# Stick-breaking attention with queries on partitions, a reversed scan in place of suffix-sum products

## Chip, cores and metric

One core of a Trainium2 chip runs the whole program. The metric is the device time of one execution in microseconds. The kernel before took 2721.27 us (median of 3 runs, 2720.59 to 2722.27).

## What is computed

The program is a chain of transformer-like layers on 512 tokens of width 1024, all in float32. The change touches one of them, the stick-breaking attention of the last mixer: 16 heads of 64 dimensions, 512 queries and keys.

```python
def stick_breaking_attention(q, k, v):
    """A[t,s] = beta_ts * prod_{s<j<t}(1 - beta_tj), s < t."""
    for i in range(seq // Q_BLOCK):              # blocks of 128 queries
        z = einsum('bqhd,bkhd->bhqk', q_block, k[:, :kv_len]) * scale
        causal = k_pos < q_pos
        log_beta = log_sigmoid(z)
        log_1m = where(causal, log_beta - z, 0.0)
        later = cumsum(log_1m, axis=3, reverse=True) - log_1m
        w = where(causal, exp(log_beta + later), 0.0)
        out = einsum('bhqk,bkhd->bqhd', w, v[:, :kv_len])
```

The weight of a key is its own sigmoid times the product of (1 - sigmoid) over all later keys before the query.

## The kernel before

The program is written engine by engine. A list of stages (`plan`) is made first, and each engine walks the list in order, issuing its own instructions and waiting on counted semaphores (`wait_ge(*at_(...))`, raised by `.then_inc(*by(...))`). Every engine runs its instructions strictly in that order, so a waiting instruction holds all that is behind it on its engine.

Most stages are large matrix products, three products on split float32 values each (L1760 to L1762), whose weights SyncE loads two units ahead, ScalarE rounds (L985) and VectorE subtracts (L1394). The attention stage `attend` stands between two of them (the query projection and the product with `b_w_o`); both weight buffers are then full, so it runs with no weight traffic.

The attention has keys on partitions. Head by head, for key blocks j = 0 to 3, with 512, 384, 256 and 128 queries (1280 columns):

- TensorE makes the scores in one of four PSUM banks `X` (L1986). A bank is taken when its last user has been read (`bank`, `freed`).
- VectorE adds the causal bias and moves them to SBUF (L1574).
- ScalarE runs Abs, Exp and Ln over all 1280 columns (L1239, L1240, L1247), each Exp and Ln with a change of its function table.
- VectorE makes softplus and log beta (L1586, L1587).
- TensorE adds up the softplus of later keys: `below` for the keys of the same block (L1996), a tile of ones for each later block (L1999), into PSUM `G`: ten fp32 products a head.
- VectorE subtracts that from log beta (L1580), ScalarE takes Exp (L1244), TensorE multiplies with the values (L2008), VectorE copies the head's output (L1591).

Heads are staggered over a loop index k: in one turn TensorE issues the scores of head k+1, the suffix sums of k-1 and the value products of k-2. An fp32 product appears as two MATMUL records in the trace; a transpose appears as one.

The constants `ident`, `upper` and `below` are made by GpSimd at the start (L915 to L929). GpSimd's work during the projections is the squares for the norms (L952). It has none in the attention. The stage after, `down`, starts when the last head's output is in `big`: ScalarE makes `u_hi` (L1263), VectorE `u_lo` (L1702).

Of the kernel before, what the change touches and what calls it, by code (L numbers as in the profile page):

```python
# [12 lines left out]
P = 128  # L13
# [114 lines left out]
def build(nc, w, out, upto=None):  # L128
# [3 lines left out]
    with ExitStack() as ctx:  # L132
# [22 lines left out]
        below = sb("below", [P, P])  # L155
# [240 lines left out]
        def plan_sb():  # L396
            s = stage("attend", akind="SB", heads=SB_HEADS, aux={}, operand=state["operand"])
            use = s.aux
            s.gfreed = [gfreed[m][-1] for m in range(4)]
            for k in range(-1, s.heads + 3):  # L400
                if k + 1 < s.heads:
                    for j in range(TT):
                        use["qk", k + 1, j] = aux("z", s.i, k + 1, j)
                        mark("z", s.i, k + 1, j)
                    mark("log_done", s.i, k + 1)
                if 1 <= k <= s.heads:
                    mark("sp", s.i, k - 1)
                    for j in range(TT):
                        mark("later", s.i, k - 1, j)
                        mark("arg", s.i, k - 1, j)  # L410
                if 2 <= k < s.heads + 2:
                    mark("exp_done", s.i, k - 2)
                    use["pv", k - 2] = aux("y", s.i, k - 2)
                    mark("y", s.i, k - 2)
            state["y"] = ("y", s.i, s.heads - 1)

# [216 lines left out]
        plan_sb()  # L633
        plan_down(8)
# [193 lines left out]
        def _(pool):  # L828
# [65 lines left out]
            def pool_s5_table():  # L894
# [7 lines left out]
                for n in (2, 4, 8, 16, 32):  # L902
# [14 lines left out]
            pool.memset(below[:, :], 1.0).then_inc(consts, 1)  # L917
            pool.wait_ge(consts, 3)
# [7 lines left out]
            pool.wait_ge(consts, 7)  # L926
            pool.tensor_copy(bias_tile[:, :], junk[:, 1, :].bitcast(I32)).then_inc(consts, 1)
            pool.wait_ge(consts, 8)
# [4 lines left out]
            for n in range(NUSED):  # L933
# [22 lines left out]
        tri_at, TRI = [0, 512, 896, 1152], 1280  # L956
        workf = work[:, :, :].rearrange("p a b -> p (a b)")

        def tri(x, j=None):
            return x[:, 0:TRI] if j is None else x[:, tri_at[j]:tri_at[j] + SEQ - P * j]  # L960

        def sb_sp(hd, j=None):
            return tri(att[:, 16:21, :].rearrange("p a b -> p (a b)")[:, TRI * (hd % 2):TRI * (hd % 2) + TRI], j)

        def sb_lb(hd, j=None):
            x = workf[:, TRI:2 * TRI] if hd % 3 == 2 else \
                big[:, 16:21, :].rearrange("p a b -> p (a b)")[:, TRI * (hd % 3):TRI * (hd % 3) + TRI]
            return tri(x, j)

        def sb_z(hd, j=None):  # L970
            return tri(workf if hd % 2 else att[:, 21:24, :].rearrange("p a b -> p (a b)"), j)
# [3 lines left out]
        def _(act):  # L975
# [25 lines left out]
            def act_slot(s, t):  # L1001
# [6 lines left out]
                if s.akind == "s5":  # L1008
                    return act_s5(s, t)
                maps, T = 2 if s.akind == "A" else 1, len(s.steps)  # L1010
# [133 lines left out]
            act.wait_ge(consts, 9)  # L1144
# [3 lines left out]
            for s in plan:  # L1148
# [83 lines left out]
                elif s.kind == "attend":  # L1232
                    for k in range(s.heads + 2):
                        if k < s.heads:
                            L = sb_lb(k)
                            if k >= 3:
                                act.wait_ge(*at_("aux_ready", s.aux["pv", k - 3]))
                            act.wait_ge(*at_("z", s.i, k, TT - 1))
                            link("act", act, nc.scalar.activation(L, sb_z(k), ACT.Abs))  # L1239
                            link("act", act, nc.scalar.activation(L, L, ACT.Exp, scale=-1.0))  # L1240
                        if k >= 2:
                            act.wait_ge(*at_("arg", s.i, k - 2, TT - 1))
                            e = sb_lb(k - 2)
                            nc.scalar.activation(e, e, ACT.Exp).then_inc(*by("exp_done", s.i, k - 2))  # L1244
                        if k < s.heads:

                            nc.scalar.activation(L, L, ACT.Ln, bias=one_c).then_inc(*by("log_done", s.i, k))  # L1247
# [39 lines left out]
        def _(dve):  # L1287
# [136 lines left out]
            def dve_slot(s, t):  # L1424
# [6 lines left out]
                if s.akind == "s5":  # L1431
                    return dve_s5(s, t)
                T = len(s.steps)
# [128 lines left out]
            def dve_sb(s):  # L1562

                link("dve", dve, V.tensor_scalar(bias_tile[:, :], upper[:, :], -BIG, BIG, ALU.mult, ALU.add))
                link("dve", dve, V.scalar_tensor_tensor(bias_tile[:, 0:P], ident[:, :], BIG, bias_tile[:, 0:P],
                                                        ALU.mult, ALU.add))
                for k in range(s.heads + 3):
                    if k < s.heads:
                        if k >= 2:
                            dve.wait_ge(*at_("sp", s.i, k - 2))  # L1570
                        for j in range(TT):
                            a = s.aux["qk", k, j]
                            dve.wait_ge(*at_("aux_ready", a))
                            V.tensor_tensor(sb_z(k, j), X[:, a % 4, 0:SEQ - P * j], bias_tile[:, 0:SEQ - P * j],  # L1574
                                            ALU.add).then_inc(*by("z", s.i, k, j))
                    if 2 <= k < s.heads + 2:
                        for j in range(TT):
                            e = sb_lb(k - 2, j)
                            dve.wait_ge(*at_("later", s.i, k - 2, j))
                            V.tensor_tensor(e, e, G[:, j, 0:SEQ - P * j], ALU.subtract)\  # L1580
                                .then_inc(*by("arg", s.i, k - 2, j))
                    if 1 <= k <= s.heads:

                        z, L = sb_z(k - 1), sb_lb(k - 1)
                        dve.wait_ge(*at_("log_done", s.i, k - 1))
                        link("dve", dve, V.scalar_tensor_tensor(sb_sp(k - 1), z, 0.0, L, ALU.max, ALU.add))  # L1586
                        V.scalar_tensor_tensor(L, z, 0.0, L, ALU.min, ALU.subtract).then_inc(*by("sp", s.i, k - 1))  # L1587
                    if k >= 3:
                        a, r = s.aux["pv", k - 3], 64 * ((k - 3) % 2)
                        dve.wait_ge(*at_("aux_ready", a))  # L1590
                        V.tensor_copy(big[r:r + 64, (k - 3) // 2, :], X[r:r + 64, a % 4, :])\  # L1591
                            .then_inc(*by("y", s.i, k - 3))
# [3 lines left out]
            for s in plan:  # L1596
# [81 lines left out]
                elif s.kind == "attend":  # L1678
                    dve_sb(s)
# [70 lines left out]
        def _(pe):  # L1750
# [22 lines left out]
            def pe_slot(s, t):  # L1773
# [6 lines left out]
                if s.akind == "s5":  # L1780
                    return pe_s5(s, t)
                T = len(s.steps)
# [35 lines left out]
                if t < T:  # L1818
# [4 lines left out]
                    for m in range(2 if s.akind == "A" else 1):  # L1823
# [10 lines left out]
                        ins.then_inc(*by("aux_ready", s.aux["qk", t, m]))  # L1834

# [63 lines left out]
            pe.wait_ge(consts, 9)  # L1899
# [8 lines left out]
            for s in plan:  # L1908
# [68 lines left out]
                elif s.kind == "attend":  # L1977
                    pe.wait_ge(*at_(*s.operand))
                    vv = att[:, 0:8, :].rearrange("p (t a) n -> p t (a n)", a=2)
                    for k in range(-1, s.heads + 2):  # L1980
                        if k + 1 < s.heads:
                            hd = k + 1
                            r = slice(64 * (hd % 2), 64 * (hd % 2) + 64)
                            for j in range(TT):
                                b = bank(s.aux["qk", hd, j])
                                pe.matmul(b[:, 0:SEQ - P * j], big[r, 8 + hd // 2, j * P:(j + 1) * P],  # L1986
# [58 lines left out]
```

## Time and profile before

| what | value |
|---|---|
| median of 3 runs | 2721.27 us |
| profiled execution | 2723.9 us, span 2722.2 us |
| TensorE busy | 2468.2 us, 91% |
| VectorE busy | 1397.0 us, 51% |
| ScalarE busy | 972.3 us, 36% |
| GpSimd busy | 226.3 us, 8% |
| chain that ended last | TensorE 83%, VectorE 9%, issue 3%, ScalarE 3% |
| mean granted TensorE clock | 0.944 |

The shares are averages over the whole program. The attention stage is 167 us of it, and its engines are loaded otherwise than the average; it has to be read by itself, from the stretch 2118 to 2286 us of the span. The granted clock is a share of 2.4 GHz: 1.00 is full speed, 0.50 is 1.2 GHz.

### The profile page before, as it was taken

The numbers are of one execution on the slowest core, as the hardware profiler recorded it, in microseconds if no ns is written. First come the engines' busy times: TensorE is split into PE (matmuls) and PEld (weight loads), VectorE is DVE, ScalarE is ACT, GpSimd is POOL, SyncE is SP. The second block draws the span as 40 slices with busy tenths as digits, with TensorE's granted clock in tenths as the row PEclk, the third lists the DMA queues.
The fourth block names the chain that finished last, engine by engine and source line by source line (L and its number), as shares of the span: only waits on it lengthen the run. The fifth ranks groups of instructions, "written<-read, shape, count | busy, mean of one in ns | idle before, by whom it ended". The sixth has DMA issues, their size and how long they took to land.

```text
span 2722.2 us, 29106 instructions
## 1 busy us (share of the span) xinstructions
PE 2468.2 (91%) x11110; PEld 1945.3 (71%) x11110; DVE 1397.0 (51%) x2851; ACT 972.3 (36%) x1312; POOL 226.3 (8%) x252
## 2 busy tenths in 40 slices
PE   4789989898799999999798989999899899899998
PEld 3567667677577676767687778878687556688877
DVE  6875575755445343443364354554444675445543
ACT  3334435332443434342313222223333775222232
POOL 6531010042010000000000000000011000000000
PEclk9889999899799999989877999999999899899999
DMA  6344112124132121214362222222222000233222
GB/s 170 111 135 124 62 48 76 47 93 139 62 93 63 62 78 47 78 47 147 117 212 67 93 78 93 93 93 83 88 89 82 1 1 31 77 94 93 93 78 93
DMA packets 191358, 233.46 MB, mean 86 GB/s; under 512 B 39455, under 2 KB 120822, under 8 KB 191222
## 3 DMA queue, kind: packets, MB, share of 16 engines
q1 hardware_dynamic: 170503, 211.05, 24.3%
q10 hardware_dynamic: 20719, 20.56, 2.5%
q8 instruction: 90, 1.47, 0.2%
q14 instruction: 46, 0.38, 0.0%
HBM read 212.69 MB, written 23.07 MB: 87 GB/s over the span
## 4 chain that ended last, share of the span: by engine, by line
PE 83%; DVE 9%; issue 3%; ACT 3%; SPq 1%; DMA 1%; ACTq 0%; POOLq 0%; DVEq 0%
PE G L1760 22%; PE G L1761 21%; PE G L1762 21%; PE X L1880 2%; PE X L1915 2%; PE G L1996 1%; ACT w_hi L985 1%; PE G L1999 1%; PE X L2008 1%; PE X L1816 1%; PE X L1769 1%; PE X L1830 1%; PE X L1986 1%; DVE w_lo L1394 1%; PE X L1804 1%
## 5 line engine op out<-in xcount | busy, mean ns | idle before, releaser
L1394 DVE TENSOR_TENSOR w_lo<-raw,w_hi 128x512 fp32r<-128x512 f32 x696 | 481.8, 734 | 613.0 <-ACT w_hi L985 612.7
L1760 PE MATMUL G<-w_hi,u_hi 128*128 128x512 f32 x1600 | 653.5, 408 | 23.2 <-issue 14.8
L1762 PE MATMUL G<-w_hi,u_lo 128*128 128x512 f32 x1600 | 633.7, 396 | 0.0
L1761 PE MATMUL G<-w_lo,u_hi 128*128 128x512 f32 x1600 | 633.3, 396 | 0.0
L985 ACT ACTIVATE w_hi<-raw 128x2048 fp32r<-128x2048 f32 (+1 forms) x176 | 333.5, 1895 | 837.6 <-PE G L1762 796.9
L1760 PE MATMUL G<-u_hi,w_hi 128*128 128x512 f32 x1120 | 450.6, 402 | 0.0
L1761 PE MATMUL G<-u_lo,w_hi 128*128 128x512 f32 x1120 | 441.8, 394 | 0.0
L1762 PE MATMUL G<-u_hi,w_lo 128*128 128x512 f32 x1120 | 441.1, 394 | 0.0
L1760 PEld LDWEIGHTS G<-w_hi,u_hi 128*128 128x128 f32 x1600 | 307.4, 192 | 108.5 <-issue 35.1
L1762 PEld LDWEIGHTS G<-w_hi,u_lo 128*128 128x128 f32 x1600 | 306.2, 191 | 67.2
L1761 PEld LDWEIGHTS G<-w_lo,u_hi 128*128 128x128 f32 x1600 | 307.5, 192 | 61.7 <-issue 0.5
L1760 PEld LDWEIGHTS G<-u_hi,w_hi 128*128 128x128 f32 x1120 | 213.6, 191 | 64.5 <-issue 18.4
L1762 PEld LDWEIGHTS G<-u_hi,w_lo 128*128 128x128 f32 x1120 | 213.5, 191 | 46.4
L1761 PEld LDWEIGHTS G<-u_lo,w_hi 128*128 128x128 f32 x1120 | 214.0, 191 | 42.3
L952 POOL TENSOR_TENSOR work<-att 128x512 f32<-128x512 f32 x68 | 76.6, 1127 | 1661.9 <-ACT att L990 1661.8
L1702 DVE TENSOR_TENSOR u_lo<-big,u_hi 128x512 fp32r<-128x512 f32 x132 | 86.3, 718 | 158.8 <-ACT u_hi L1263 158.8
L1915 PE MATMUL X<-ident,att 128*128 128x128 f32 x256 | 48.6, 370 | 101.9 <-DVE att L1603 99.4
L1915 PEld LDWEIGHTS X<-ident,att 128*128 128x128 f32 x256 | 43.7, 197 | 107.6 <-DVE att L1603 102.4
L1042 ACT ACTIVATE att<-att,small 128x128 f32<-128x128 f32 (+3 forms) x112 | 62.5, 559 | 131.0 <-DVE small L1461 130.9
L1024 ACT ACTIVATE att<-X 128x128 f32<-128x128 f32 (+2 forms) x112 | 46.9, 419 | 134.9 <-PE X L1816 134.9
L1816 PE MATMUL X<-ident,att 128*128 128x128 f32 x264 | 49.1, 280 | 37.7 <-DVE work L1490 21.5
L1457 DVE CUSTOM_DVE_ANT_0 att<-X,bias_tile 128x128 f32<-128x128 f32 (+3 forms) x48 | 23.5, 489 | 108.7 <-PE X L1830 108.7
(292 smaller groups left out, 2472.3 us busy)
## 6 DMA issues: line engine op xcount, KB each, us to landing
raw<-in_ffn_w_up SPq DMA_DIRECT2D x88, 512.0 KB, 4.7
raw<-in_e_w_in SPq DMA_DIRECT2D x56, 512.0 KB, 4.7
raw<-in_o_w_in SPq DMA_DIRECT2D x56, 512.0 KB, 4.5
raw<-in_ffn_w_down SPq DMA_DIRECT2D x40, 512.0 KB, 4.6
raw<-in_e_w_out SPq DMA_DIRECT2D x16, 512.0 KB, 4.5
raw<-in_o_w_out SPq DMA_DIRECT2D x16, 512.0 KB, 4.5
raw<-in_a_w_glu SPq DMA_DIRECT2D x16, 512.0 KB, 4.0
raw<-in_w_kv SPq DMA_DIRECT2D x16, 512.0 KB, 4.3
```

Source lines behind the costliest of these rows:

```text
L952: pool.tensor_tensor(sq[:, m, :], x, x, ALU.mult).then_inc(*by("q_squared", s.i, m))
L985: nc.scalar.activation(w_hi[:, n % HL, 0:kn], raw[:, n % RAW, 0:kn], ACT.Copy).then_inc(w_hi_done, 1)
L1024: nc.scalar.activation(att[:, 20:20 + nb, i * P:(i + 1) * P], X[:, a % 4, 0:nb * P].rearrange("p (a b) -> p a b", b=P), ACT.Copy).then_inc ...
L1042: ins = nc.scalar.activation(S, src, ACT.Exp, bias=nmx[:, c:c + 1], accum_out=rs[:, c:c + 1])
L1394: V.tensor_tensor(w_lo[:, n % HL, k], raw[:, n % RAW, k], w_hi[:, n % HL, k].bitcast(F32), ALU.subtract).then_inc(w_lo_done, 1)
L1702: V.tensor_tensor(u_lo[:, 4 * (l % 2) + j, :], big[:, k, :], u_hi[:, 4 * (l % 2) + j, :].bitcast(F32), ALU.subtract).then_inc(*by("u_ready ...
L1760: pe.matmul(out, lh, rh, start=start, stop=False)
L1761: pe.matmul(out, lh, rl, start=False, stop=False)
L1762: return pe.matmul(out, ll, rh, start=False, stop=stop)
L1816: ins = pe.transpose(b[:, j * P:(j + 1) * P], S[:, j * P:(j + 1) * P], ident[:, :])
L1880: ins = pe.matmul(b[a][:, NSUP * g + 1:NSUP * g + NSUP], Z[r, c, g, :], S[r, c, g, 0:NSUP - 1], start=False, stop=g == 3 and c == 1)
L1915: ins = pe.transpose(b[:, t * P:(t + 1) * P], xn_view[:, t, k * P:(k + 1) * P], ident[:, :])
```

## The change

Queries lie on partitions, keys on columns. There are 64 steps of (head, block i of 128 queries), over L = 128 (i+1) keys. ScalarE takes two Sigmoids of the scores straight from PSUM: of -z (`sb_keep`, 1 minus beta) and of z (`sb_take`, beta). VectorE runs `tensor_tensor_scan` from the last key to the first, state = max(keep x state, bias); the bias is 0 except in the diagonal block, where it is 1 at and after the query. GpSimd zeroes beta at and after the query in the diagonal block. VectorE multiplies beta by the product of the next key on. TensorE transposes the weights block by block into `G`, ScalarE copies them to SBUF, and after a head's fourth step TensorE multiplies with the values and VectorE copies the output. The suffix-sum products, `below`, Abs, Exp, Ln and the bias additions are gone.

The stage is now of kind `between` with a host of 69 slots. In slot t the queues are: TensorE scores of t, transposes of t-3, value products if t-4 is a head's last step; ScalarE both Sigmoids of t, copy of t-3; VectorE scan and product of t, output copy if t-5 is a last step; GpSimd the select of t.

```diff
-        below = sb("below", [P, P])
+        def sb_keep(t):
+            return att[:, 16 + t % 3, :]
+        def sb_prod(t):
+            return work[:, 4 + t % 2, :]
+        def sb_take(t):
+            return big[:, 16 + t % 4, :]
+        def sb_turned(hd):
+            return work[:, 0:4, :] if hd % 2 else att[:, 20:24, :]
 @block.gpsimd
-            pool.memset(below[:, :], 1.0).then_inc(consts, 1)
-            pool.affine_select(out=below[:, :], in_=below[:, :], compare_op=ALU.is_gt, fill=0.0, base=0,
-                               pattern=[[-1, P]], channel_multiplier=1).then_inc(consts, 1)
+                if n == sb_down.n:
+                    for t, (hd, i) in enumerate(sb_mix.steps):
+                        d = sb_take(t)[:, P * i:P * i + P]
+                        pool.wait_ge(*at_("sb_take", sb_mix.i, t))
+                        pool.affine_select(out=d, in_=d, compare_op=ALU.is_gt, fill=0.0, base=0, pattern=[[-1, P]],
+                                           channel_multiplier=1).then_inc(*by("sb_masked", sb_mix.i, t))
+            def act_sb(s, t):
+                T = len(s.steps)
+                if t < T:
+                    hd, i = s.steps[t]
+                    a, L = s.aux["qk", t], P * (i + 1)
+                    act.wait_ge(*at_("aux_ready", a))
+                    if t >= 3:
+                        act.wait_ge(*at_("sb_product", s.i, t - 3))
+                    nc.scalar.activation(sb_keep(t)[:, 0:L], X[:, a % 4, 0:L], ACT.Sigmoid, scale=-1.0)\
+                        .then_inc(*by("sb_keep", s.i, t))
+                    if t >= 4:
+                        act.wait_ge(*at_("sb_turned", s.i, t - 4))
+                    nc.scalar.activation(sb_take(t)[:, 0:L], X[:, a % 4, 0:L], ACT.Sigmoid)\
+                        .then_inc(*by("sb_take", s.i, t))
+                if 0 <= t - 3 < T:
+                    hd, i = s.steps[t - 3]
+                    if hd >= 2 and i == 0:
+                        act.wait_ge(*at_("aux_ready", s.aux["pv", hd - 2]))
+                    act.wait_ge(*at_("sb_turned", s.i, t - 3))
+                    nc.scalar.activation(sb_turned(hd)[:, 0:i + 1, i * P:(i + 1) * P],
+                                         G[:, (t - 3) % 4, 0:(i + 1) * P].rearrange("p (a b) -> p a b", b=P),
+                                         ACT.Copy).then_inc(*by("pt_copied", s.i, t - 3))
+            def dve_sb(s, t):
+                T = len(s.steps)
+                if t == 0:
+                    link("dve", dve, V.memset(bias_tile[:, 0:384], 0.0))
+                    link("dve", dve, V.tensor_copy(bias_tile[:, 384:512], upper[:, 0:P]))
+                if t < T:
+                    i = s.steps[t][1]
+                    L = P * (i + 1)
+                    dve.wait_ge(*at_("sb_keep", s.i, t))
+                    V.tensor_tensor_scan(sb_prod(t)[:, 0:L][:, ::-1], sb_keep(t)[:, 0:L][:, ::-1],
+                                         bias_tile[:, 384 - P * i:512][:, ::-1], 1.0, ALU.mult, ALU.max)\
+                        .then_inc(*by("sb_product", s.i, t))
+                    dve.wait_ge(*at_("sb_product", s.i, t))
+                    dve.wait_ge(*at_("sb_masked", s.i, t))
+                    w_ = sb_take(t)[:, 0:L - 1]
+                    V.tensor_tensor(w_, w_, sb_prod(t)[:, 1:L], ALU.mult).then_inc(*by("p_ready", s.i, t))
+                if is_last(s, t - 5):
+                    hd = s.steps[t - 5][0]
+                    a, q = s.aux["pv", hd], 64 * (hd % 2)
+                    dve.wait_ge(*at_("aux_ready", a))
+                    V.tensor_copy(big[q:q + 64, hd // 2, :], X[q:q + 64, a % 4, :]).then_inc(*by("y", s.i, hd))
+            def pe_sb(s, t):
+                T = len(s.steps)
+                if t < T:
+                    hd, i = s.steps[t]
+                    b, L = bank(s.aux["qk", t]), P * (i + 1)
+                    r = slice(64 * (hd % 2), 64 * (hd % 2) + 64)
+                    pe.matmul(b[:, 0:L], att[r, 8 + hd // 2, i * P:(i + 1) * P], big[r, 8 + hd // 2, 0:L],
+                              start=True, stop=True).then_inc(*by("aux_ready", s.aux["qk", t]))
+                if 0 <= t - 3 < T:
+                    i = s.steps[t - 3][1]
+                    pe.wait_ge(*at_("p_ready", s.i, t - 3))
+                    pe.wait_ge(*at_("sb_masked", s.i, t - 3))
+                    pe.wait_ge(*(at_("pt_copied", s.i, t - 7) if t >= 7 else at_(*s.gfreed[t - 3])))
+                    for j in range(i + 1):
+                        ins = pe.transpose(G[:, (t - 3) % 4, j * P:(j + 1) * P], sb_take(t - 3)[:, j * P:(j + 1) * P],
+                                           ident[:, :])
+                    ins.then_inc(*by("sb_turned", s.i, t - 3))
+                if is_last(s, t - 4):
+                    hd = s.steps[t - 4][0]
+                    pe.wait_ge(*at_("pt_copied", s.i, t - 4))
+                    b = bank(s.aux["pv", hd])
+                    for j in range(TT):
+                        ins = pe.matmul(b[r, P * j:SEQ], vv[:, j, 64 * hd:64 * hd + 64], sb_turned(hd)[:, j, P * j:SEQ],
+                                        start=j == 0, stop=j == TT - 1)
+                    ins.then_inc(*by("aux_ready", s.aux["pv", hd]))
```

## Rows read from the trace of the kernel before

**Rows 1.** Windows of the attention stage: window, length, busy us (instructions) per engine, PEclk, DMA, GB/s.
```profile
core 0: us, PE busy (x) PEld busy (x) DVE busy (x) ACT busy (x) POOL busy (x), PEclk, DMA share, GB/s
2118.66:2285.92 167.26, 152.77 (x576) 92.11 (x576) 113.71 (x176) 124.90 (x97) 0.00 (x0) 0.96 0.00 1
2147.99:2262.10 114.11, 111.76 (x426) 67.64 (x427) 83.41 (x132) 92.88 (x72) 0.00 (x0) 0.99 0.00 1
```

**Rows 2.** Chain of waits in one steady head: start, us, what, records.
```profile
2244.75 2.35 PE X L1986 x8
2247.10 1.05 PE G L1996 x2
...
2250.76 0.43 PE G L1996 x2
2251.64 2.30 PE X L2008 x8
```

**Rows 3.** The same chain, transposes before the stage and a table load.
```profile
2107.19 0.45 PE X L1769 x4
...
2114.21 3.69 PE X L1769 x16
...
2122.89 1.28 ACT L1240
```

**Rows 4.** Groups of instructions by form: count, busy us, mean ns, idle before.
```profile
L1024 ACT ACTIVATE att<-X 128x512 f32<-128x512 f32 x20 | 11.9, 597 | 33.2 <-PE X L1816 33.2
L1024 ACT ACTIVATE att<-X 128x128 f32<-128x128 f32 x20 | 5.5, 277 | 53.0 <-PE X L1816 53.0
L1229 ACT ACTIVATE att<-G 128x256 f32<-128x256 f32 x16 | 6.1, 384 | 29.7 <-PE G L1762 29.7
L1051 ACT ACT_TABLE_LOAD x1 | 1.3, 1283 | 9.8 <-issue 9.8
L1580 DVE TENSOR_TENSOR big<-big,G 128x512 f32<-128x512 f32 x11 | 7.6, 688 | 17.7 <-PE G L1999 17.7
L1580 DVE TENSOR_TENSOR big<-big,G 128x128 f32<-128x128 f32 x11 | 3.1, 279 | 0.0
L921 POOL TENSOR_SCALAR_AFFINE_SELECT upper<-upper 128x512 f32<-128x512 f32 x1 | 0.6, 612 | 0.0
L923 POOL TENSOR_SCALAR_AFFINE_SELECT below<-below 128x128 f32<-128x128 f32 x1 | 0.3, 292 | 0.0
L1880 PE MATMUL X<-work,att 64*128 64x63 f32 x256 | 43.1, 375 | 0.0
```

**Rows 5.** Single lines: duration in ns as least, median, most, and first and last start.
```profile
L1690 DVE TENSOR_TENSOR_SCAN big<-att x1: 1212/1212/1212, 745.2 to 745.2; 12x512 f32<-12x512 f32 x1
L952 POOL TENSOR_TENSOR work<-att x68: 1038/1040/1557, 61.0 to 2109.0; 128x512 f32<-128x512 f32 x68
```

**Rows 6.** Timeline: start, us of the merged run, engine, line, operation, count.
```profile
1363.25 1.42 DVE L1543 TENSOR_TENSOR_SCAN work<-big,work 128x256 f32<-128x256 f32 x2
2099.35 2.13 DVE L1394 TENSOR_TENSOR w_lo<-raw,w_hi 128x512 fp32r<-128x512 f32 x2
2099.39 1.55 POOL L952 TENSOR_TENSOR work<-att 128x512 f32<-128x512 f32 x1 [13.58 <-ACT att L990]
2285.23 0.69 DVE L1591 COPY big<-X 64x512 f32<-64x512 f32 x1 [1.18 <-PE X L2008]
2286.62 4.91 DVE L1702 TENSOR_TENSOR u_lo<-big,u_hi 128x512 fp32r<-128x512 f32 x8 [0.69 <-ACT u_hi L1263]
```

**Rows 7.** Windows of two stretches at a lower granted clock, columns as in rows 1.
```profile
2176.00:2184.00 8.00, 7.61 (x22) 4.19 (x21) 4.95 (x8) 7.69 (x6) 0.00 (x0) 0.79 0.01 1
1404.00:1460.00 56.00, 51.19 (x323) 49.79 (x323) 25.10 (x42) 9.35 (x16) 0.00 (x0) 0.50 0.40 118
```

**Rows 8.** Windows before, during and after sixteen transposes, columns as in rows 1.
```profile
2111.00:2114.20 3.20, 0.00 (x0) 0.00 (x0) 2.83 (x13) 0.00 (x0) 0.00 (x0) 0.51 0.00 0
2114.20:2117.90 3.70, 3.68 (x16) 3.27 (x16) 2.39 (x5) 2.06 (x3) 0.00 (x0) 0.50 0.00 0
2118.00:2122.00 4.00, 3.34 (x12) 1.94 (x13) 1.89 (x5) 1.00 (x2) 0.00 (x0) 1.00 0.00 0
```

More of the change, by code:

```diff
@@ L396, in plan_sb, with plan_sb_slot @@
         def plan_sb():
-            s = stage("attend", akind="SB", heads=SB_HEADS, aux={}, operand=state["operand"])
-            use = s.aux
+            s = Stage("attend", akind="SB", heads=SB_HEADS, aux={}, operand=state["operand"])
+            s.i = ("attention", "SB", len(plan))
+            s.steps = [(hd, i) for hd in range(s.heads) for i in range(TT)]
+            s.slots = len(s.steps) + 5
             s.gfreed = [gfreed[m][-1] for m in range(4)]
[L400 to L414, printed above, removed]
-            state["y"] = ("y", s.i, s.heads - 1)
+            stage("between", host=s, host_at=0, host_end=s.slots)
+            for t in range(s.slots):
+                plan_sb_slot(s, t)
+            state["y"] = ("y", s.i, s.heads - 1)
+            return s
+        def plan_sb_slot(s, t):
+            T = len(s.steps)
+            if t < T:
+                s.aux["qk", t] = aux("sb_take", s.i, t)
+                mark("sb_keep", s.i, t)
+                mark("sb_take", s.i, t)
+                mark("sb_masked", s.i, t)
+                mark("sb_product", s.i, t)
+                mark("p_ready", s.i, t)
+            if 0 <= t - 3 < T:
+                mark("sb_turned", s.i, t - 3)
+                mark("pt_copied", s.i, t - 3)
+            if is_last(s, t - 4):
+                hd = s.steps[t - 4][0]
+                s.aux["pv", hd] = aux("y", s.i, hd)
+                mark("y", s.i, hd)
         def plan_down(kt, first=0, host=None, host_at=0, y=None):
@@ L1231, in _ @@
                         w_high(n + 2)
[L1232 to L1247, printed above, removed]
                 elif s.kind == "forget":
@@ L1560, in dve_s5 @@
                         .then_inc(*by("u_ready", s.i, k))
[L1562 to L1592, printed above, removed]
@@ L1781, in pe_slot @@
                     return pe_s5(s, t)
+                if s.akind == "SB":
+                    return pe_sb(s, t)
                 T = len(s.steps)
@@ L1976, in _ @@
                     ins.then_inc(*by("aux_ready", s.aux))
[L1977 to L1986, printed above, removed]
-                                          att[r, 8 + hd // 2, j * P:SEQ], start=True, stop=True)\
-                                    .then_inc(*by("aux_ready", s.aux["qk", hd, j]))
-                        if 1 <= k <= s.heads:
-                            g = k - 1
-                            pe.wait_ge(*at_("sp", s.i, g))
-                            for j in range(TT):
-                                pe.wait_ge(*at_(*(("arg", s.i, g - 1, j) if g else s.gfreed[j])))
-                                b = G[:, j, :]
-                                ins = pe.matmul(b[:, 0:SEQ - P * j], below[:, :], sb_sp(g, j), start=True,
-                                                stop=j == TT - 1)
-                                for i in range(j + 1, TT):
-                                    ins = pe.matmul(b[:, P * (i - j):SEQ - P * j], ones[:, :], sb_sp(g, i),
-                                                    start=False, stop=i == TT - 1)
-                                ins.then_inc(*by("later", s.i, g, j))
-                        if k >= 2:
-                            g = k - 2
-                            pe.wait_ge(*at_("exp_done", s.i, g))
-                            b = bank(s.aux["pv", g])
-                            r = slice(64 * (g % 2), 64 * (g % 2) + 64)
-                            for j in range(TT):
-                                ins = pe.matmul(b[r, P * j:SEQ], vv[:, j, 64 * g:64 * g + 64], sb_lb(g, j),
-                                                start=j == 0, stop=j == TT - 1)
-                            ins.then_inc(*by("aux_ready", s.aux["pv", g]))
                 elif s.kind == "between":
```

43 lines of the change are left out of this document (22 added, 21 removed).

## The prediction
> **What bounds the kernel now.** I read the page's shares first (TensorE 91% busy, 83% of the chain of waits), then windows of the one stage that the change rewrites, then the chain inside it. The stage runs from the first score product at 2118.66 to the end of the last head's output copy at 2285.92: 167.26 us, of which TensorE is busy 152.77, ScalarE 124.90, VectorE 113.71, GpSimd 0, with no DMA to speak of [rows 1]. In its steady part TensorE is busy 111.76 of 114.11 us, and those twelve heads give 9.51 us a head. The chain there is TensorE's own sequence [rows 2]: four score products (eight records) 2.35 us; the suffix sums, from 2247.10 to the start of the value products at 2251.64, 4.54 us; the value products 2.30 us; every second head a 0.7 us wait of the score products for a bank that VectorE's copy frees. So TensorE bounds this stage, and nearly half of its time there is the suffix sums. What lies around the 16 heads is the filling (no TensorE work in some of 2119 to 2146) and the emptying (2262 to 2286).
>
> **What goes, what comes, on each engine.** Per head, four steps of 128 queries against 128, 256, 384 and 512 keys, 1280 columns in all, as many as before.
>
> *TensorE.* Gone: 10 fp32 products (20 records) for the suffix sums, 4.54 us. The score and value products keep their shapes and counts (only which operand is stationary changes), 2.35 and 2.30 us. New: 1+2+3+4 = 10 transposes of 128x128. The trace has the same operation: four take 0.45 us at full clock, 0.11 each, and sixteen take 3.69 us at half clock, 0.23 each [rows 3]. Ten cost 1.1 us. Sum: 2.35 + 2.30 + 1.1 = 5.75 us a head.
>
> *ScalarE.* Gone: per head four passes over 1280 columns and two table loads of 1.28 us. New: three passes over the four pieces, two Sigmoids and one copy, all read from PSUM, and no table change between them. Such a pass takes 0.277 us for 128 columns and 0.597 for 512, and a Sigmoid of 256 columns 0.384, on the same line [rows 4]; the four pieces sum to 1.75 us, three times that is 5.2 us. One table load remains, at the first Sigmoid.
>
> *VectorE.* Gone: the bias additions, the subtractions and the two 1.49 us passes per head. New: per step one scan, a wait for it, and one product. The trace has the scan at 512 columns (1.212 us, on 12 partitions) and at 256 columns on 128 partitions, where two linked ones take 1.42 us, thus 0.69 each with 0.036 between [rows 5, 6]: 2.04 ns a column. Four: 0.43 + 0.69 + 0.95 + 1.21 = 3.28, with links 3.43 us. A two-input product takes 0.279 us at 128 and 0.688 at 512 columns, and eight of 512 without a wait take 4.91 us, a pitch of 0.60, 0.083 below the duration [rows 4, 6]. Four products cost 1.93 - 4 x 0.083 = 1.60 us; the output copy, 0.69 us long [rows 6], costs 0.60 at that pitch. Sum 5.63 us a head. That the scan reads and writes backwards appears in no row: I bound it by no change below and by twice the scan, 2.6 us more a head, above; I take no change, since the row nearest is a scan of the same types, and keep the other end as a rival.
>
> *GpSimd.* New: one select on 128x128 per step, 0.292 us when alone [rows 4]; 1.2 us a head, far from a bound. But it shares something with VectorE. GpSimd's square of 128x512 takes 1.04 us at the median; the one at 2099.39, issued while VectorE ran a two-input subtraction, took 1.55 us, and the VectorE pair around it took 2.13 us where two at that pitch take 1.29: VectorE lost 0.84 us, about as long as the square's own columns, and GpSimd lost 0.5, the rest of VectorE's instruction [rows 5, 6]. Both new VectorE operations have two SBUF inputs. A select streams 128 columns; from 0.292 us for 128 and 0.612 for 512 columns its own columns take 0.107 us [rows 4]. So I charge VectorE 4 x 0.107 = 0.43 us a head. Bounds: 0 (it falls into the gap between scan and product), and 4 x 0.292 = 1.17. VectorE then needs 6.06 us a head, and it is the new bound, with TensorE 0.3 behind and ScalarE 0.8 behind.
>
> **Does the order of the queues let VectorE run through?** Slots are 3 deep. VectorE's product of step t needs the select of t, behind both Sigmoids of t; ScalarE's Sigmoids of t stand behind its copy of step t-4, which needs TensorE's transposes of t-4, which need VectorE's product of t-4. Worst place: TensorE's value products (2.30 us) stand ahead of the next head's 128-query scores and of the transposes of its second step. From the end of the product of step 0 of a head: transposes and value products until 2.5, score 2.8, first Sigmoid 3.2; VectorE comes to that scan only after steps 1, 2, 3 and the copy, 5.3 us. About 2 us to spare; the steps of 256, 384 and 512 keys have as much or more. GpSimd waits at most one scan (1.2 us) for its turn and still comes before the product. The output copy needs the value products 3.2 us after the same instant and stands behind some 5 us of work. So what is late next is VectorE alone. TensorE waits for it about 1 us in one stretch of each head. I still allow 0.15 us a head, 2.4 us, for waits between queues.
>
> **The stage after.** Filling: score of 128 queries 0.5, table load 1.28, Sigmoid 0.28, passing between engines 0.2: 2.25 us until VectorE starts (the table load as it appears in the chain [rows 3]). Then 16 x 6.06 - 0.60 = 96.4. Emptying: transposes 0.65 with passing, copy 0.7, value products 2.4, output copy 0.75: 4.5. With the allowance 105.5 us, against 167.3: 61.8 less.
>
> **The rest.** A memset and the select of `below` (0.29 us) leave GpSimd's first 5 us; ScalarE's first table load only comes after 9.8 us in which nothing of GpSimd holds it [rows 4], so nothing is gained, 0.5 us at most. The 64 selects stand in GpSimd's queue behind the last squares, with nothing behind them. The bias preparation stays two small VectorE operations before the scores. SyncE has nothing to move here: both weight buffers are full before the stage. The next stage starts from the last output copy as before.
>
> The sum goes by the profiled execution: 2723.9 (span 2722.2 and 1.7 around it) - 61.8 = 2662.1. The median of the runs, 2721.3, lies 2.6 below the profiled one: 2659.5, so 2660.
>
> **Rivals.** (a) *TensorE's clock sinks once in each head.* The work that remains is score products on 64 rows, value products on 64 columns, and transposes, with a wait of about 1 us a head. For: before, between 2176 and 2184, the clock was 0.79 with TensorE busy 7.61 of 8 us, and from 1404 to 1460 it stayed at 0.50, the 1.2 GHz level, with TensorE busy 51.2 of 56 us, with products of 64 and 63 columns [rows 4, 7]. Against: it was 0.99 over the steady 114 us [rows 1], and transposes raised it: 0.51 in the idle stretch before them, 0.50 during 3.7 us of nothing else, 1.00 right after [rows 8]. A mean of 0.79 over those 8 us is 3.4 us at half clock, which costs 1.7 us of TensorE time; one such stretch in every head, less the 0.3 to spare, 1.4 x 16 = 22 us: 2682.
>
> (b) *VectorE is dearer.* The backward scan at twice the time: 16 x 2.6 = 42 us, 2702. The select at 0.292 each instead of 0.107: 0.74 x 16 = 12 us, 2672.
>
> (c) *Slower: TensorE at 1.2 GHz throughout the stage.* Then 2 x 5.75 = 11.5 us a head, TensorE is the bound again, 184 + some 9 at the ends = 193 us, 26 more than before: 2747. It turns slower from about 10 us a head, a half-clock share of some 85% of the stage. Against: with TensorE the bound it would have no waits, and full columns follow each other, the condition in which the clock rose in rows 8; the stretch at 1404 had half as many columns to each weight load.
> The Trainium skill, "TensorE: Matmul & The Clock Gate", Part 4 (PE-mode transpose), says that transposes do not count as TensorE activity and so do not engage the full clock. By it each head would have 1.1 us more of "idle" beside its wait, which speaks for (a), or at worst (c), and the sum would be 2682 or 2747. The trace disagrees in the one place that shows transposes alone, the sixteen of rows 3 and 8, and I follow the trace.
>
> (d) *Cheaper.* Selects wholly hidden and no waits: 7 + 2.4 us less, 2650.
>
> **Chances.** Forecast (2650 to 2668) 0.60; (a) 0.18; (b) 0.12; (c) 0.04; (d) below 2650 0.04; a mishap that leaves the time within 0.2% of before 0.02. The range for 8 in 10 takes the forecast, (a) and the cheap half of (b): 2648 to 2690. A change under 0.2% (5.4 us) couldn't be told from none. Faster 0.94, within 0.01, slower 0.05.
>
> **What would show it.** In the new profile: the stage at about 105 us; VectorE busy over 95% of its steady part, scans of 1.21 us at 512 columns (2.3 would be (b)); some products or scans 0.1 us longer where a select runs; TensorE about 0.9 busy with short waits for VectorE's product, its clock near 1.0 (under 0.85 would be (a)); ScalarE about 85%. Wrong would be a chain in which TensorE or ScalarE holds most of the stage, or scans that wait for a Sigmoid in every step.

## The result, and the profile after

The changed kernel took 2671.26 us (median of 4 runs, 2666.25 to 2674.13) against 2721.77 before (four runs by now): ratio 0.9814, 95% interval 0.9801 to 0.9827. The profiled execution took 2668.6 us, span 2666.8. I had said 2660, range 2648 to 2690.

The stage first. It runs from the first score product at 2112.22 to the end of the last output copy at 2232.23, 120.0 us, where [rows 1] had 167.3 and I had said 105.5. Windows of the changed kernel (columns as in rows 1): the low-clock stretch around the stage's start, and its steady part.

```profile
core 0: us, PE busy (x) PEld busy (x) DVE busy (x) ACT busy (x) POOL busy (x), PEclk, DMA share, GB/s
2103.50:2130.80 27.30, 22.25 (x54) 11.65 (x55) 16.32 (x35) 12.58 (x27) 4.70 (x9) 0.50 0.00 1
2130.80:2225.00 94.20, 94.20 (x355) 44.29 (x356) 78.50 (x123) 60.87 (x166) 35.31 (x55) 1.00 0.00 1
```

In the steady part TensorE is busy all 94.20 us, VectorE 78.50 (83%), ScalarE 60.87. TensorE still bounds the stage; I had named VectorE. Before the steady part the granted clock is 0.50 for 27 us, 18.6 of them inside the stage. The chain of waits over one steady head answers to rows 2:

```profile
2158.08 0.41 PE X L1858 x2
2158.49 0.37 PE G L1866 x2
2158.86 0.62 PE X L1858 x2
2159.49 0.48 PE G L1866 x3
2159.97 0.84 PE X L1858 x2
2160.80 0.59 PE G L1866 x4
2161.39 1.05 PE X L1858 x2
2162.45 0.26 PE G L1866
2162.71 2.30 PE X L1876 x8
```

L1858 are the scores, L1866 the transposes, L1876 the value products. One head is 6.93 us (6.92 as a mean of many): scores 0.41 + 0.62 + 0.84 + 1.05 = 2.92 where [rows 2] had 2.35 for the same eight records, transposes 0.37 + 0.48 + 0.59 + 0.26 = 1.70 for ten where I had 1.1 from [rows 3], value products 2.30 as before. The step from one score group to the next is 0.21 us, the price of 128 columns; what is left in each is 0.20. The transposes are 0.11 each and 0.15 on top in each group. So each time TensorE goes from one kind of product to the other it loses 0.15 to 0.20 us, eight times a head, 1.4 us, of which the one switch into the scores (0.2) was already in my 2.35. A ninth one, into the value products, is in their 2.30, as it was before: their columns alone need 2.13.

The timeline shows where the loss sits. The weight loads (PEld) at two such switches of the changed kernel come first. Below them is the switch from value products to scores in the kernel before, load and product:

```profile
2165.72 0.29 PEld L1858 LDWEIGHTS X<-big,att 64*128 64x128 f32 x2 [0.17 <-issue]
2166.34 0.31 PEld L1866 LDWEIGHTS G<-ident,big 128*128 128x128 f32 x3 [0.33 <-issue]
```
```profile
2206.65 0.29 PEld L1986 LDWEIGHTS X<-att,big 64*128 64x128 f32 x2 [0.17 <-issue]
2206.66 0.69 PE L1986 MATMUL X<-att,big 64*128 64x512 f32 x1
```

The load starts with its product and not ahead of it (2206.65 and 2206.66): the weight load stands on the path. The tile shape, rows by columns of the weights, changes there: from 128 by 64 to 64 by 128 at this last switch, and between 64 by 128 and 128 by 128 at the two above. The Trainium skill, "TensorE: Matmul & The Clock Gate", Part 2 (what each phase is for), says that TensorE pulls a weight load ahead of the running product when the row groups don't conflict or the load goes to the background buffer. The traces agree with it inside a group of one shape: four transposes in a row take 0.11 us each with loads of 0.14 us. At a change of shape they show no pull-ahead.

VectorE's operations, and GpSimd's select, by form (mean ns after the busy us):

```profile
L1592 DVE TENSOR_TENSOR_SCAN work<-att,bias_tile 128x512 f32<-128x512 f32 x16 | 19.5, 1219 | 1.5 <-ACT att L1067 1.4
L1592 DVE TENSOR_TENSOR_SCAN work<-att,bias_tile 128x256 f32<-128x256 f32 x16 | 11.8, 737 | 0.2
L1598 DVE TENSOR_TENSOR big<-big,work 128x511 f32<-128x511 f32 x16 | 11.1, 692 | 3.1 <-POOL big L975 3.1
L975 POOL TENSOR_SCALAR_AFFINE_SELECT big<-big 128x128 f32<-128x128 f32 x64 | 40.8, 639 | 82.4 <-ACT big L1071 82.4
```

The backward scan takes 1.22 us at 512 columns, as the forward one of [rows 5] did. The select takes 639 ns in the mean where it took 292 alone [rows 4]. One that starts beside a scan shows why:

```profile
2163.25 1.22 DVE L1592 TENSOR_TENSOR_SCAN work<-att,bias_tile 128x512 f32<-128x512 f32 x1
2163.64 0.92 POOL L975 TENSOR_SCALAR_AFFINE_SELECT big<-big 128x128 f32<-128x128 f32 x1 [0.97 <-ACT big L1071]
```

It ends at 2164.56, 0.09 us after the scan; the one beside the scan of 384 columns ends 0.09 us after that, too.

Of the 55.4 us between the two spans, 47.3 are the stage, 1.7 what follows it, and 6.4 lie ahead of it, in code that the change touches only by the two instructions of `below`. That part is taken up under `e_below`.

### The profile page after: what moved, and what is told of

Read it like the earlier page. It is cut to its first block, busy times and chain, and to the rows that moved or that the text cites. A ratio compares the mean times of both kernels' runs of the same rounds, so it can differ in the third digit from the quotient of the medians.

```text
span 2666.8 us, 29121 instructions
## 1 busy us (share of the span) xinstructions
PE 2428.4 (91%) x10950; PEld 1905.4 (71%) x10950; DVE 1380.5 (52%) x2819; ACT 921.4 (35%) x1408; POOL 267.7 (10%) x314
## 4 chain that ended last, share of the span: by engine, by line
PE 84%; DVE 8%; issue 3%; ACT 3%; SPq 1%; DMA 1%; ACTq 0%; POOL 0%; DVEq 0%; POOLq 0%
PE G L1771 23%; PE G L1773 22%; PE G L1772 22%; PE X L1858 2%; PE X L1924 2%; PE X L1959 2%; PE X L1876 1%; ACT w_hi L991 1%; PE X L1829 1%; PE X L1780 1%; PE X L1843 1%; PE G L1866 1%; PE X L1846 1%; PE X L1817 1%; PE X L1842 1%
```

## The experiments

The theory after the first trace: TensorE loses an unhidden weight load at each change of tile shape, and starts the stage at half clock. Heads below are the spacing of the output copies in the steady part, stages go from first score to the end of the last copy. In the cuts of the edits `...` stands for lines left out.

**The changed kernel again, and with the unused tile back.** `a_same` is the same program; `e_below` differs by

```diff
+        below = sb("below", [P, P])
...
+            pool.memset(below[:, :], 1.0).then_inc(consts, 1)
+            pool.affine_select(out=below[:, :], ...).then_inc(consts, 1)
...
```

> The changed kernel itself, run again. In its first trace the attention takes 120 us: 16 heads at 6.93 us with TensorE busy throughout, and a first stretch to 2130.8 at half clock, which I put at some 7 us. Theory A (the low clock at the start of the stage is chance of when the clock rises): the time spreads over several us from run to run, 2664 to 2675, and the low stretch at the start has another length in this trace. Rival (the spread comes from elsewhere): the start of the stage looks the same and the time differs in another place.

> The changed kernel with the unused tile `below` back: its place in SBUF, its memset and its select. The changed kernel reached the attention 6.4 us earlier than the kernel before, 0.7 of it at the first weights, though nothing else in front of the stage was changed. Theory (the two GpSimd instructions stand on the starting path, and the rest is the clock falling and rising at other moments): first weights 0.7 us later again, and the attention starts somewhere within some us of the kernel before's. Rival (chance from run to run): the start of the attention differs from the first trace by as much in the unchanged program.

Measured: 2669.17 (2661.86 to 2671.84) and 2671.10 (2668.66 to 2673.76). Both heads 6.92, both stages 119.7 us, both at half clock for 23.9 us, from 1.5 us ahead of the last transposes before the stage. The first score came at 2116.0 and at 2113.1, where it was 2112.2 in the first trace and 2118.7 before. So `below` is not the cause, neither of the 6.4 us nor of the earlier first weights (with it back, they came 1.2 us before the old time); in the seven traces with the changed kernel's code ahead of the stage the first score comes between 2112.2 and 2118.0 (`e_pairs`), so that the old 2118.7 lies hardly outside of what one code shows. Against my expectation for `a_same` the low stretch at the start was nearly the same (27.3 and 23.9 us) and the stage the same to 0.3 us; the difference between the two traces lies ahead of the stage. The time is to be read by medians and the stage by itself.

**Scores over 128 rows.** `e_rows128`:

```diff
-                    r = slice(64 * (hd % 2), 64 * (hd % 2) + 64)
+                    r = slice(0, 128)
```

> The score products read all 128 rows of the query and key tiles instead of the head's 64 (the scores are then the sum of two heads', so the output is not the reference's). Columns and records are the same. Theory (TensorE loses 0.15 to 0.20 us of unhidden weight load each time when consecutive products differ in their rows or columns, 64x128 against 128x128, eight times a head): the head falls from 6.93 to about 5.6 us of TensorE work, VectorE becomes the bound at 6.1 to 6.3, the stage loses 10 to 13 us: 2658. Rival 1 (the loss comes from the switch between product and transpose, whatever the shape): nothing changes, 6.93 a head. Rival 2 (the loss comes from the semaphore waits ahead of each group): nothing changes either.

Measured: 2654.81 (2653.12 to 2656.46), ratio 0.9755 (0.9740 to 0.9769), head 6.09, stage 102.2. The chain over one head:

```profile
2154.49 0.42 PE X L1858 x2
2154.91 0.22 PE G L1866 x2
2155.13 0.43 PE X L1858 x2
2155.56 0.33 PE G L1866 x3
2155.89 0.65 PE X L1858 x2
2156.54 0.44 PE G L1866 x4
2156.97 0.04 issue
2157.01 1.13 PE X L1858 x2
2158.13 0.11 PE G L1866
```

In every other head the chain leaves TensorE once:

```profile
2148.36 0.43 PE X L1858 x2
...
2148.82 0.28 ACT att L1067
2149.10 0.18 ACT big L1071
...
2149.33 0.47 POOL big L975
...
2149.90 0.30 DVE big L1598
...
2150.22 0.69 DVE big L1605
...
2150.96 1.13 PE X L1858 x2
```

Two transposes 0.22, three 0.33, four 0.44, one 0.11: nothing is lost between products and transposes once both are 128x128. The first scores, behind value products of 64 columns, still cost 0.42 for 0.21 of columns, and the 512-key scores 1.13 for 0.85: those stand behind a real wait, for the bank that VectorE's output copy (L1605) frees. This decides for the shape and against both rivals: products and transposes alternate as before, and all semaphore waits are in place. With 1.2 us less TensorE would need some 5.75 us a head; the head fell by 0.83 to 6.09, and the rest is that wait. TensorE still has four fifths of the chain and is busy 59.25 of 60 us, VectorE 56.62.

The stage fell by 17.6 us against `a_same`, more than 16 x 0.83 = 13.3. The clock has a part in it. With nothing changed but the rows of the scores it was back at 1.00 in 4.3 us from the first score, where `a_same` took 17.9; it had gone down 1.5 us ahead of the transposes in both:

```profile
2116.90:2121.10 4.20, 3.35 (x19) 2.15 (x18) 3.78 (x7) 3.93 (x12) 2.24 (x5) 1.00 0.00 0
```

The other two traces with scores over 128 rows and a half clock at the start of the stage show 4.3 (`v_padk`) and 4.9 us (`v_padk_tele`), the other five with 64 rows and no added products 14.5 to 18.6. What follows the stage took 437.1 us in this trace and 434.3 in `a_same`, so that the whole gained less than the stage.

**Pairs.** `e_pairs` issues two steps' scores in a row, `e_pairs2` puts the value products between the scores and the transposes (the comments are not in the kernels):

```diff
-                if t < T:
+                for t_ in (t, t + 1) if t % 2 == 0 else ():                       # e_pairs
+                for t_ in ((0,) if t == 0 else (t, t + 1) if t % 2 else ()):      # e_pairs2: scores
...
+                for t_ in (t - 3, t - 2) if t % 2 else ():                        # e_pairs2: transposes, last
...
```

> TensorE issues the scores of two steps and then the transposes of two steps, so four switches a head go away, two into scores at 0.20 and two into transposes at 0.15. Shape theory and rival 1 alike: 6.93 - 0.70 = 6.23 us a head, 11 us less in all, 2660. Rival 2 (each wait costs, not each switch): the waits are as many as before, so 6.93 a head and no gain. If VectorE already binds at 6.2 to 6.4, the head stays there.

> Again the scores of two steps together and the transposes of two steps together, but now with the value products between the two groups, so that they no longer stand right behind the transposes whose copies they need (in e_pairs the head took 7.27 us, with TensorE busy 54.4 of 60 us and waits of the value products for ScalarE's copy and of the scores for VectorE's). Theory (a switch costs 0.15 to 0.20, and two of the eight pairs of switches are gone): 6.93 - 0.70 = 6.23 us a head, 2658 to 2662. Rival (a pair holds the queues back wherever it stands, since scores are issued a step too early and a bank comes free late): over 6.6 us a head.

Measured: `e_pairs` 2679.92 (one of its four runs took 10,555 us, for a reason that no trace shows; the others 2676.3 to 2680.2), head 7.27, stage 122.7; `e_pairs2` 2666.96 (2660.20 to 2669.34), head 6.43, stage 110.6. The first missed: in its trace TensorE is busy 54.36 of 60 us, and the weight loads of the value products wait for ScalarE's copy (10.7 us between 2130 and 2220), those of the scores for the bank that VectorE's output copy frees (8.8 us). Four switches a head went, and waits worth more than they came. In the second:

```profile
2140.00:2200.00 60.00, 56.53 (x239) 28.26 (x239) 54.86 (x85) 39.24 (x112) 18.39 (x38) 1.00 0.00 1
```

TensorE is busy 56.53/60 x 6.43 = 6.06 us a head against 6.92, so the switches gave back 0.86 where they were priced at 0.70; the head stops at 6.43 since the chain now passes through ScalarE's Sigmoid and copy. The reorder frees TensorE and makes a new wait; over half of the gain is left in the head. The stage is 9.1 us shorter than in `a_same`, but the median gains only 2 to 4 us: in this trace what follows the stage took 438.9 us instead of 434.3, with stretches at half clock (around 2230 and 2535) that the changed kernel's trace does not have there. Whether the reorder brings them about is open.

**Clock.** `v_warm`, in the idle stretch before the last transposes:

```diff
+                    if s.owed.i == sq_last.i:
+                        pe.wait_ge(*at_("staged", sq_last.i, 0))
+                        for _ in range(7):
+                            pe.matmul(G[:, 0, :], ident[:, :], upper[:, :], start=True, stop=True)
```

> The changed kernel with seven fp32 products of 128x512 on constants in TensorE's 6.6 us idle stretch ahead of the last transposes before the attention; nobody reads them. Theory (the half clock over the first 18 to 20 us of the stage costs 7 to 9 us, because the mix of small products there does not lift it once it has sunk): the clock stays at 1.00 into the stage, the transposes take 1.9 us instead of 3.7, the first value products come about 9 us after the first scores instead of 13.4, and the time falls by 7 to 10 us to about 2661. Rival (the mix itself pulls the clock down): the clock sinks again within the stage, and nothing is gained.

Measured: 2667.05 (2664.57 to 2670.99), head 6.92, stage 117.4. The windows of its stage:

```profile
2112.00:2117.40 5.40, 4.42 (x17) 2.39 (x18) 3.54 (x7) 5.33 (x15) 2.27 (x5) 1.00 0.00 0
2117.40:2127.60 10.20, 10.20 (x21) 3.93 (x20) 6.71 (x10) 3.30 (x8) 2.21 (x3) 0.50 0.01 2
```

The clock was up at the start and sank at 2117.4 after 5.4 us in which TensorE was busy 4.42; then 10.2 us at half. So both were partly right: the products held the clock up to the stage, and in its first steps it sank. The stage gained 2.4 us, not 7 to 10.

**Weights as differences.** `v_tele` uses that beta x P[k+1] = P[k+1] - P[k] for the scan's output P:

```diff
-                    nc.scalar.activation(sb_take(t)[:, 0:L], X[:, a % 4, 0:L], ACT.Sigmoid)
...
-                        pool.affine_select(out=d, in_=d, ...).then_inc(*by("sb_masked", sb_mix.i, t))
...
-                    V.tensor_tensor(w_, w_, sb_prod(t)[:, 1:L], ALU.mult)
+                    V.tensor_tensor(sb_take(t)[:, 0:L - 1], sb_prod(t)[:, 1:L], sb_prod(t)[:, 0:L - 1], ALU.subtract)
...
```

> The weights taken as differences of neighbouring products (beta x P[k+1] = P[k+1] - P[k], P the scan's output), so the second Sigmoid and all 64 selects are gone and VectorE shares nothing with GpSimd. Theory (TensorE's switches bind, VectorE and ScalarE are off the path): the head stays at 6.93 us; up to 2 us less at the two ends of the stage. My prediction's picture (VectorE binds, the selects cost it 0.43 us a head): 0.4 to 0.7 us less a head, 7 to 11 us in all.

Measured: 2669.36 (2669.06 to 2670.09), head 6.92, stage 119.8. One of ScalarE's three passes a step and all of GpSimd's selects are gone, and the head is as long as before: both are shown off the path.

**The select, where VectorE is near its bound.** `e_nosel` is `e_rows128` without the selects:

```diff
-                        pool.affine_select(out=d, in_=d, compare_op=ALU.is_gt, ...)
...
-                    dve.wait_ge(*at_("sb_masked", s.i, t))
+                    dve.wait_ge(*at_("sb_take", s.i, t))
```

> The kernel with scores over 128 rows and without the 64 selects of GpSimd (so weights at and after the query in the diagonal block are not zeroed; the scores are sums of two heads' too). VectorE is near its bound there, 6.09 us a head. Theory of the prediction (a select takes 0.107 us of VectorE's time, 0.43 a head): 5.7 to 5.9 us a head, 3 to 6 us less than e_rows128. Rival (the select delays by its chain, Sigmoid to select to product, only where VectorE has caught up, and shares nothing that matters): the same 5.9 in the heads but scans and products as long as before. Second rival (ScalarE and the banks hold the head at 6.09): no change.

Measured: 2652.18 (2650.12 to 2653.12), head 5.89, stage 98.6. The scan of 512 columns, in `e_rows128` and here:

```profile
L1592 DVE TENSOR_TENSOR_SCAN work<-att,bias_tile 128x512 f32<-128x512 f32 x16 | 20.9, 1303 | 0.0
```
```profile
L1585 DVE TENSOR_TENSOR_SCAN work<-att,bias_tile 128x512 f32<-128x512 f32 x16 | 19.5, 1216 | 0.0
```

It was 87 ns longer beside the selects, near the 107 that I charged for each, but the other forms hardly moved (951 against 950 at 384 columns). The idle time before the 128-column products, waiting for the select, fell from 2.8 to 0.5 us in the whole stage, 0.14 a head. The head lost 0.20 us, half of my 0.43, and the two terms, 0.09 of sharing and 0.14 of waiting, would account for it; they were not told apart. In `e_rows128` the select stands on the chain in every other head, ahead of the output copy for which TensorE waits, so that the expectation's rival, the delay by the chain, holds at least in part. TensorE is busy 60.00 of 60 us here, so a further gain would not show.

**A version with all of it.** `v_padk` gets 128 rows with the full result: GpSimd fills the other head's rows of a key tile with zeros during the query projection. `v_padk_tele` adds the differences, `v_all` the seven products as well.

```diff
+                if n == sq_first.n:
...
+                    for c in range(8):
+                        do(pool.tensor_copy(big[64:128, c, :], big[64:128, 8 + c, :]))
+                        do(pool.memset(big[64:128, 8 + c, :], 0.0))
+                        ins = pool.memset(big[0:64, c, :], 0.0)
...
+                    pe.matmul(b[:, 0:L], att[:, 8 + hd // 2, i * P:(i + 1) * P], sb_k(hd)[:, 0:L],
```

> Scores on 128 rows with the full result: GpSimd makes for each head a key tile whose other 64 rows are zero, while the query projection runs (8 copies and 16 memsets of 64x512, some 13 us of an idle engine, which may hold VectorE's two-input instructions there by up to 4 us off the path). Shape theory: as with e_rows128, 6.1 us a head, 2655 to 2658. Rival (zeros and the copies cost as much as they bring): 2665 or more.

> Both: padded keys and weights as differences. TensorE needs 2.35 + 1.1 + 2.3 and two switches of 0.1 to 0.15, 5.9 us a head; VectorE 5.63. Theory (VectorE and its waits for the selects bind once the switches are gone, e_rows128 had 6.09 a head): now 5.8 to 5.95, 2 to 5 us less than v_padk. Rival (the waits of 6.09 come from the bank that VectorE's output copy frees): the head stays at about 6.1.

> Padded keys, weights as differences, and the seven products of 128x512 in TensorE's idle stretch ahead of the stage. Theory: 5.89 us a head as in v_padk_tele, and the clock at 1.00 when the stage starts; in v_warm that was worth 2.4 us of the stage, since the clock sank again for 10 us soon after. 2646 to 2650. Rival (with full 128-row scores the mix keeps the clock up once it is up): no half clock in the stage at all, 4 to 6 us less than v_padk_tele: 2644 or less.

| kernel | median us | ratio to before (95%) | head | stage |
|---|---|---|---|---|
| `v_padk` | 2657.14 | 0.9757 (0.9741 to 0.9774) | 6.09 | 102.1 |
| `v_padk_tele` | 2649.87 | 0.9738 (0.9724 to 0.9753) | 5.89 | 99.2 |
| `v_all` | 2650.47 | 0.9730 (0.9716 to 0.9745) | 5.89 | 98.6 |

```profile
2112.10:2210.80 98.70, 95.18 (x416) 53.42 (x416) 90.76 (x144) 52.73 (x130) 0.00 (x0) 1.00 0.00 1
```

That is the whole stage of `v_all`: the clock stays at 1.00, with the same seven products that held it only 5 us in `v_warm`. The pipeline has to fill in `v_all` as in `v_warm`, so the filling alone does not bring the clock down. Together with `e_rows128` this speaks for the scores of 64 rows as the cause, though `v_all` also takes the weights as differences. Yet against `v_padk_tele` (half clock until 4.9 us into the stage) the stage is only 0.6 us shorter; why so little is not shown. The two best are equal in what these runs can tell, both some 20 us below the changed kernel. TensorE (95.18) and VectorE (90.76) are now both near full. `v_padk` landed in its expected 2655 to 2658; `v_padk_tele` gained 7 us on it where 2 to 5 were expected; for `v_all` the rival's clock came, not its 2644.

## Why the prediction was right, and where it was off

The direction and the mechanism of the saving held: the suffix sums, 4.54 us a head, left the engine that bounds the stage, and nothing in the new steps ran serially. The time lay 11 us above the forecast, beyond its own 2650 to 2668 and inside the range. That it lay inside owes something to luck: the range was widened for rivals (a) and (b), and neither is what used that room. The prediction's own sign of being wrong came true, too: TensorE holds the chain in the whole stage. By its steps:

- *TensorE, 5.75 us a head.* This step failed in size: 6.93. Value products were 2.30 as said, scores 2.92 for 2.35, transposes 1.70 for 1.1. I took durations from runs of one shape, where weight loads are hidden, and put them into a sequence that changes shape at every group. A sign of it stood in [rows 2]: the first suffix sum behind the scores takes 1.05 us where its two records of 512 columns need 0.85. `e_rows128` showed the cause. (6.93 - 6.06) x 16 = 13.9 us is nearly the whole gap of the stage, 120.0 against 105.5.
- *VectorE is the new bound at 6.06.* Wrong in this kernel, by that same term. The scans were as priced, backward as forward (rival b fell). In `e_rows128` the head came to 6.09, but that it is so near to 6.06 proves nothing: VectorE is busy 56.62/60 x 6.09 = 5.75 us of it, and TensorE holds most of the chain. The chain is VectorE's in `v_padk_tele`, at 5.89.
- *Select 0.43.* Nothing in the changed kernel's head. Where VectorE was nearly full, sharing and the wait for the select together made 0.20; the sharing that the scans show is 0.09 a head.
- *Queues let the bound engine run through.* Right: 94.20 of 94.20 us, though for TensorE. There was little to spare in them: `e_pairs`, with every second score a step earlier, brought waits.
- *Filling and emptying, 6.8 us and 2.4 of allowance, at full clock.* The half clock of rival (a) came, once and at the start, not in each head. With it shortened the stage gained 2.4 us (`v_warm`) and 0.6 (`v_all`). What 18.6 us at half clock cost the changed kernel was not measured by itself. An estimate: beside sixteen steady heads its stage has 120.0 - 16 x 6.92 = 9.3 us, that of `e_rows128` 102.2 - 16 x 6.09 = 4.8, so some 4 to 5 us. The prediction had 105.5 - 16 x 6.06 = 8.5 there, so the allowance for waits that didn't come paid for a half clock that did: luck.
- *Transposes lift the clock [rows 8].* Not borne out in the changed kernel. The same sixteen transposes ran at half clock after 2107.8 in the changed kernel, and the clock stayed down for 19 us behind them, in `a_same` and `e_below` likewise. But in `e_nosel`, where nothing ahead of the stage was changed, it rose at their end, as in the kernel before:

```profile
2108.60:2111.70 3.10, 0.00 (x0) 0.00 (x0) 2.72 (x13) 0.00 (x0) 0.00 (x0) 0.50 0.00 0
2111.70:2115.40 3.70, 3.67 (x16) 3.28 (x16) 2.38 (x5) 2.06 (x3) 0.00 (x0) 0.50 0.00 0
2115.40:2119.40 4.00, 2.99 (x12) 1.65 (x11) 1.51 (x4) 3.92 (x9) 0.00 (x0) 0.99 0.00 0
```

  That is two of the eleven traces that have these transposes in a half-clock stretch. The Trainium skill, "TensorE: Matmul & The Clock Gate", Part 4, says that transposes don't count. The nine without a rise agree with it, these two speak against it, and the runs don't settle it; a rise there can't be counted on.
- *`below` gains nothing.* Right, shown by `e_below`.
- *Around the stage.* I took it as unchanged. The medians differ by 50.5 us, the stages by 47.3, what follows by 1.7; 1.5 us are left, within what identical code ahead of the stage showed from trace to trace, and whether any of it is due to the change stays open. These 3.2 us made the miss of the whole smaller than the 14.5 us of the stage.

## What to carry to other kernels

Price a sequence of small products by the order in which they will stand, not by the sum of their durations: look in the trace for the start of the first product after a change of rows or columns, and charge that gap at each change. An operand padded with zeros to the neighbour's shape can be cheaper than the half-size product. When a bound is moved, the next one may be the same engine with another loss; work taken from the others is worth nothing until it is gone.

## What the runs showed of the hardware

- A change between TensorE tiles of 64x128, 128x128 and 128x64 rows by columns costs 0.15 us (into 128 rows) to 0.20 us (into the scores) at full clock (2158.08 to 2165.01 of the changed kernel). Alternating products and transposes of one shape cost nothing (`e_rows128`: 0.22, 0.33, 0.44 us for two, three and four transposes), unless the product stood behind a real wait. Rows and columns were not told apart beyond the value products: their change of columns alone, 64 to 128, cost 0.21.
- A product over 64 rows takes as long as one over 128: 128 more columns are 0.21 us more in both (0.41, 0.62 and 0.84 us in the changed kernel, 0.43 and 0.65 in `e_rows128`).
- A GpSimd select of 128x128 took 0.29 us alone. In the changed kernel it took 0.64 in the mean and up to 0.93; the one of 0.92 started beside a scan and ended 0.09 us after it. How busy VectorE is does not decide it: the mean was 0.37 in `e_rows128`, with VectorE at 94%. There VectorE's long scan took 87 ns more than without selects.
- Once down before the stage, the clock stayed at half for 20 to 27 us in the six traces with scores of 64 rows, and for 7 to 14 us in the four with scores of 128 rows. In `v_warm`, where it sank only inside the stage, it was 10.2 us.
